# A two-layer decoder trunk whose stages overlap by token pair: the last gate/up pieces run for one pair first, and norms, pool mixer and sums of a pair run in the other pair's products

## The reference

```python
def modulate(x, g, mod):
    shift, scale, gate = jnp.split(mod, 3, axis=-1)
    h = rmsnorm(x, g) * (1.0 + scale[:, None, :]) + shift[:, None, :]
    return h, gate[:, None, :]
...
#   x += 1/2 * gate * SwiGLU_1(h);  x += gate * Mixer_l(h);  x += 1/2 * gate * SwiGLU_2(h)
def swiglu(h, w_in, w_out):            # D_FF = 2816
    g, u = jnp.split(h @ w_in, 2, axis=-1)
    return (jax.nn.silu(g) * u) @ w_out
...
def mixer_pool(h, w_grp, scale):       # layer 1; 4 channel groups, windows 2, 4, 8, 16
    ...
        p = ((cg - prev) / cnt).astype(h.dtype) - h[..., sl]   # trailing mean minus the token itself
        outs.append(p @ w_grp[i])
    return jnp.concatenate(outs, axis=-1) * scale
```

## Time and profile before

| | us |
|---|---|
| three runs | 2209.69, 2346.18, 2266.74 |
| median of the three | 2266.74 |
| the profiled execution | 2222.29 |
| its span on the slowest core (7) | 2220.7 |
| its span on core 3, the shortest | 2178.5 |
| busy on core 7: PE, DVE, ACT, POOL | 2081.5, 1314.5, 749.5, 609.8 |

### The profile page before, as it was taken

One profiled execution on the slowest core, in us unless ns is written; L12 is line 12 of the kernel. 1 busy time (PEld: TensorE's weight loads), 2 busy tenths in 40 slices (PEclk: granted clock), 3 DMA queues, 4 the chain that ended last, 5 costly groups with the idle time before them and its releaser, 6 DMA issues.

```text
span 2220.7 us, 30634 instructions; the slowest of 8 cores (2178.5 to 2220.7 us)
## 1 busy us (share of the span) xinstructions
PE 2081.5 (94%) x9537; PEld 930.7 (42%) x9537; DVE 1314.5 (59%) x2222; ACT 749.5 (34%) x1186; POOL 609.8 (27%) x602
## 2 busy tenths in 40 slices
PE   7999999999999899999998999999976599999996
PEld 1344444445534344444443444444433244444443
DVE  1664665666777675575766765656555554444446
ACT  2630321355225630230347311303234632130333
POOL 0041340501102052250520431423535334052320
PEclk9999999999999999999999999999988799999998
DMA  9443361542342064371450551533400024023123
GB/s 275 116 99 63 95 142 31 130 87 39 75 118 55 13 140 86 76 142 34 119 105 1 115 123 44 123 72 86 76 1 1 10 39 76 1 48 57 29 48 152
DMA packets 65438, 174.60 MB, mean 79 GB/s; under 512 B 6912, under 2 KB 7040, under 8 KB 63872
## 3 DMA queue, kind: packets, MB, share of 16 engines
q0 software_dynamic: 21744, 79.18, 21.1%
q1 hardware_dynamic: 43536, 93.46, 13.9%
HBM read 243.39 MB, written 8.39 MB: 113 GB/s over the span
## 4 chain that ended last, share of the span: by engine, by line
PE 80%; DVE 7%; issue 5%; ACT 5%; DMA 2%; POOL 1%; SPq 1%; DVEq 0%; ACTq 0%; POOLq 0%
PE ps L253 80%; DVE TP L253 4%; ACT TP L253 1%; ACT TSUM L253 1%; DMA ACTB<-wm 1%; ACT H L253 1%; DVE X L253 1%; DVE ACTB L253 1%; DVE TSUM L253 1%; DVE WMOD L253 1%; ACT L253 1%; SPq L253 1%; DMA WMOD<-wmod 1%; DVE ps L253 0%; POOL CB L253 0%
## 5 line engine op out<-in xcount | busy, mean ns | idle before, releaser
L253 PE MATMUL ps<-H,SLIN 128*128 128x512 f16 x2240 | 554.2, 393 | 18.6 <-DVE ps L253 12.8
L253 PE MATMUL ps<-ACTB,SLOUT 128*128 128x512 f16 x2368 | 529.0, 384 | 8.4 <-DVE TP L253 4.6
L253 DVE SCALAR_TENSOR_TENSOR X<-ps,GH,X 128x512 f32<-128x512 f32 x448 | 332.6, 749 | 338.7 <-PE ps L253 337.3
L253 PE MATMUL ps<-TSUM,SLIN 128*128 128x512 f16 x2016 | 509.9, 389 | 20.5 <-ACT ps L253 13.1
L253 ACT ACTIVATE TP<-ps 128x512 f32<-128x512 f32 x568 | 337.5, 598 | 402.4 <-PE ps L253 363.1
L253 POOL TENSOR_TENSOR SLIN<-SLIN 128x512 f16<-128x512 f16 x336 | 442.3, 1337 | 105.7 <-DMA SLIN<-wp 47.9
L253 PEld LDWEIGHTS ps<-ACTB,SLOUT 128*128 128x128 f16 x2368 | 233.2, 99 | 294.0 <-issue 37.2
L253 POOL DMA_DIRECT2D SLIN<-wp x91 | 51.0, 561 | 1108.3 <-PE ps L253 1098.5
L253 PEld LDWEIGHTS ps<-H,SLIN 128*128 128x128 f16 x2240 | 223.1, 100 | 306.4 <-issue 94.9
L253 ACT ACTIVATE ps<-ps 128x512 f32<-128x512 f32 x168 | 97.9, 583 | 735.0 <-PE ps L253 728.9
L253 PEld LDWEIGHTS ps<-TSUM,SLIN 128*128 128x128 f16 x2016 | 199.0, 100 | 278.2 <-issue 88.2
(11 more groups left out here) (82 smaller groups left out, 852.8 us busy)
## 6 DMA issues: line engine op xcount, KB each, us to landing
WMOD<-wmod SPq DMA_DIRECT2D x256, 256.0 KB, 4.1
SLIN<-wp POOLq DMA_DIRECT2D x91, 512.0 KB, 6.8
SLOUT<-wp POOLq DMA_DIRECT2D x60, 512.0 KB, 11.7
X<-xT SPq DMA_DIRECT2D x8, 1024.0 KB, 29.3
outT<-ACTB SPq DMA_DIRECT2D x4, 2048.0 KB, 6.3
H<-wm SPq DMA_DIRECT2D x4, 1024.0 KB, 12.0
ACTB<-wm SPq DMA_DIRECT2D x3, 1024.0 KB, 22.5
ACTB<-wm SPq DMA_DIRECT2D x2, 512.0 KB, 23.7
```

What stands on the lines that cost most here:

```text
L253: return lambda E: getattr(E, name)(*a, **k)
```

## The change

The two pairs of tiles are made to overlap across sub-layers.

- The last pieces of the last group (NLATE: 5, 5, 7 and 3 of the 7 for the four FFNs) run for pair 0 first (part l0); then tiles 0 and 1 get their output projection; then the same pieces run for pair 1 (l1, in reverse order where more than three), then tiles 2 and 3. Likewise the first pieces (NEARLY: 5, 5 and 8) of the FFNs but the first run for pair 0 (e0) and then for pair 1 (e1). In (1,2), e0 is the whole first group, and the outputs of tiles 0 and 1 come ahead of e1.
- A piece that is used in both passes is loaded and summed again if a slot was taken from it in between. Chain plans the loads into the three slots over the whole sequence of items and gives up the piece whose next use is farthest. The four FFNs load and sum 101 pieces where 84 were summed before; the SLIN loads become about 112 (91 before), POOL's sums 404 (336).
- What pair 0 needs next (norm, pool mixer, token sums) goes into a queue BG, whose steps run at six hooks in each item of pair 1, and one to three per chunk of the output projection.
- Norms: squares by 128x1024, rstd kept in TSUM, the product with rstd by 128x1024 into the input's place, then scale and shift in place, half on ACT and half on DVE.
- Pool mixer: X is cast to f16 by eight DMAs on POOL's queue; the norm's scale goes into the weights and rstd into the copy of the grouped product; the statistics come from ACT's squares and matmuls of one column. The shift of (1,1), which the pooling cancels but for rounding, is not computed: 16 of 256 w_mod steps go. POOL's 64 squares go.
- The final norm is written in place and stored by two chunks (512 KB each).
- In the middle group three w_mod steps stand in an item, and none while BG holds work. The four SLOUT loads are issued ahead of l0, not at its end.

The diff, cut to its core:

```diff
+    class Chain:
...
+            fut = self.seq[idx:]
+
+            def use(p):
+                return fut.index(p) if p in fut else 10 ** 6
...
+            for p in fut:
+                if p in seen:
+                    continue
+                seen.append(p)
...
+                        break
+                    self.drop(v)
+                slot = self.free.pop(0)
+                self.res[p] = slot
+                load_piece(p, slot, after)
+                self.pend.append(p)
+                if len(seen) > 4:
+                    break
+            for p in old:
+                self.pend.remove(p)
+                s_sums(p)
+
+        def drop(self, p):
+            self.free.append(self.res.pop(p))
+            piece_slot.pop(p, None)
...
 
     def mod_step():
+        if mod_next[0] == 96:
+            mod_next[0] = 104
...
-    def rstd_from(b, rs=None, tmr=None):
...
+    def rstd_ops(ts, bs):
+        for t, b in zip(ts, bs):
+            rs, k = rs_of(t)
+            add("act", I("activation", out=rs, in_=PS[b][:], func=AF.Ln, scale=1.0 / D, bias=EPSB[:, 0:1]),
+                reads=[("ps", b), "EPSB"], writes=k)
+            BK.give(b)
+        for t in ts:
+            rs, k = rs_of(t)
+            add("act", I("activation", out=rs, in_=rs, func=AF.Exp, scale=-0.5), reads=k, writes=k)
+
+    def stat_units(t):
+        sq_pair(t, 0)
+        yield
+        sq_pair(t, 2)
+        yield
+        sq_pair(t, 4)
...
-    def apply_gen(l, s, t, rs, tmr=None):
+        ones_pair(t, 0, b)
+        sq_pair(t, 6)
+        yield
+        ones_pair(t, 2, b)
+        yield
+        ones_pair(t, 4, b)
+        yield
+        yield
+        ones_pair(t, 6, b)
+        return b
...
+    def apply_units(l, s, t, nact):
...
+        rs, rk = rs_of(t)
+
+        def norm(c):
+            add("dve", I("tensor_tensor", out=role.hbuf[:, c:c + 2, tsl(t)], in0=X[:, c:c + 2, tsl(t)],
+                         in1=rs.unsqueeze(1).broadcast_to([128, 2, TT]), op=ALU.mult),
+                reads=[Xk(c, t), Xk(c + 1, t)] + rk, writes=[(role.hn, c, t), (role.hn, c + 1, t)])
+
+        def aff(x):
+            v = role.hbuf[:, x, tsl(t)]
+            k = (role.hn, x, t)
+            if (x * nact) % 8 < nact:
+                add("act", I("activation", out=v, in_=v, func=AF.Identity, scale=AS[:, o + x:o + x + 1], bias=MODT[:, sh + x:sh + x + 1]),
+                    reads=[k, ("AS", l, s), ("MODF", l, s)], writes=[k])
+            else:
+                add("dve", I("tensor_scalar", out=v, in0=v, scalar1=AS[:, o + x:o + x + 1], scalar2=MODT[:, sh + x:sh + x + 1],
+                             op0=ALU.mult, op1=ALU.add), reads=[k, ("AS", l, s), ("MODF", l, s)], writes=[k])
+        for c in range(0, NC, 2):
+            norm(c)
             yield
+            aff(c)
+            aff(c + 1)
+            yield
+
+    def head_units(l, s, ts, nact=4):
+        bs = []
+        for t in ts:
+            b = yield from stat_units(t)
+            bs.append(b)
+        rstd_ops(ts, bs)
+        yield
+        yield
+        for t in ts:
+            yield from apply_units(l, s, t, nact)
 
     def tv(p, n, c):
...
                 hook()
                 g.p7()
                 if mod:
...
+                if mod and nmod > 2:
+                    mod()
                 hook()
                 self.prev = g
 
...
-    def ffn_prefetch(l, i, n=3):
...
-    NEARLY = 3
...
+    NEARLY = {(0, 2): 5, (1, 0): 5, (1, 2): 8}
+    NLATE = {(0, 0): 5, (0, 2): 5, (1, 0): 7, (1, 2): 3}
...
+            ne = NEARLY[(l, s)]
+            P["e0"] = one(l, s, 0, range(ne), 0)
+            P["e1"] = one(l, s, 0, reversed(range(ne)) if ne > 3 else range(ne), 1)
+            P["g0"] = both(l, s, 0, range(ne, n0))
+        P["g1"] = both(l, s, 1, range(len(GROUPS[1])))
+        P["g2"] = both(l, s, 2, range(n2 - nl))
+        P["l0"] = one(l, s, 2, range(n2 - nl, n2), 0)
+        P["l1"] = one(l, s, 2, reversed(range(n2 - nl, n2)) if nl > 3 else range(n2 - nl, n2), 1)
...
+    def wout_load(l, s, g):
+        for dp in range(4):
+            load_piece(("wout", l, s // 2, g, dp), 3 + dp)
...
+    def out_t(l, s, t, g, nu, split=False):
...
+        for dch in range(d0, NC):
+            b = BK.take()
+            mms(dch, b, order)
+            post(dch, b)
+            PIPE.flush()
+            BG.step(nu)
...
+        def mod():
+            if BG.q:
+                return
+            if mod_next[0] < (72 if (l, s) == (0, 0) else 144):
+                mod_step()
+            elif (l, s) == (1, 0):
+                next(pm_const_ops, None)
...
+        pairs = not P["g0"]
+        if P["e0"]:
+            cut = len(P["e0"]) - (4 if pairs else 0)
+            PIPE.run(P["e0"][:cut], BG.step)
+            if pairs:
+                wout_load(l, s, 0)
+                PIPE.run(P["e0"][cut:], BG.step)
                 mod_finalize_gate(l, s)
-            if g < 2:
-                for t in range(NT):
...
+                for t in (0, 1):
+                    out_t(l, s, t, 0, 3, t == 0)
+            BG.drain()
+        PIPE.run(P["e1"], BG.step, mods)
+        if pairs:
+            for t in (2, 3):
+                out_t(l, s, t, 0, 1, t == 2)
+        else:
+            split = max(0, len(P["g0"]) - 4)
+            PIPE.run(P["g0"][:split], BG.step, mods)
+            wout_load(l, s, 0)
+            PIPE.run(P["g0"][split:], BG.step, mods)
+            mod_finalize_gate(l, s)
+            for t in range(NT):
+                out_t(l, s, t, 0, 1)
+        for g in (1,):
+            PIPE.run(P["g1"][:10], BG.step, mods, 3)
+            wout_load(l, s, 1)
+            PIPE.run(P["g1"][10:], BG.step, mods, 3)
+            for t in range(NT):
+                out_t(l, s, t, 1, 1)
+        PIPE.run(P["g2"], BG.step, mods)
+        wout_load(l, s, 2)
+        PIPE.run(P["l0"][:-2], BG.step, mods)
+        nxt.prep()
+        PIPE.run(P["l0"][-2:], BG.step, mods, quiet=True)
+        nu = 3 if (l, s) == (1, 0) else 2
+        for t in (0, 1):
+            out_t(l, s, t, 2, nu, t == 0)
+            nxt.ready(t)
+        PIPE.run(P["l1"], BG.step, quiet=True)
+        for t in (2, 3):
+            out_t(l, s, t, 2, nu, t == 2)
+            nxt.ready(t)
...
-    def pm_core_gen(l, s, t):
...
+    def pool_units(p):
+        ts = (2 * p, 2 * p + 1)
+        for t in ts:
+            for h in range(2):
+                cs = slice(4 * h, 4 * h + 4)
+                add("pool", I("dma_start", out=H[:, cs, tsl(t)], in_=X[:, cs, tsl(t)]),
+                    reads=[Xk(c, t) for c in range(4 * h, 4 * h + 4)], writes=[Hk(c, t) for c in range(4 * h, 4 * h + 4)], dma=("PX", t, h))
...
+            ss(i)
+            if i + 2 < 8:
+                sq(i + 2)
+            yield
...
-    def pm_stage2(tail_fn, ln, sn):
...
-    def final_apply_gen(t, rs):
...
+    def final_units(t):
+        b = yield from stat_units(t)
+        rstd_ops([t], [b])
+        rs, rk = rs_of(t)
         for c in range(NC):
-            add("dve", I("scalar_tensor_tensor", out=Ov[ob][:, c, :], in0=X[:, c, tsl(t)], scalar=SM[:, SM_FG + c:SM_FG + c + 1],
-                         in1=TP[:, rs, 0:TT], op0=ALU.mult, op1=ALU.mult),
-                reads=[Xk(c, t), "SM", ("TP", rs)], writes=[("O", ob, c)] + O_KEYS[ob])
-            yield
-        add("sp", I("dma_start", out=outT_v[t], in_=Ov[ob][:]), reads=[("O", ob, c) for c in range(NC)] + O_KEYS[ob], dma=("OUT", ob))
+            add("dve", I("scalar_tensor_tensor", out=X[:, c, tsl(t)], in0=X[:, c, tsl(t)], scalar=SM[:, SM_FG + c:SM_FG + c + 1],
+                         in1=rs, op0=ALU.mult, op1=ALU.mult),
+                reads=[Xk(c, t), "SM"] + rk, writes=[Xk(c, t)])
+            if c % 2:
+                add("sp", I("dma_start", out=outT_v[t][:, c - 1:c + 1, :], in_=X[:, c - 1:c + 1, tsl(t)]),
+                    reads=[Xk(c - 1, t), Xk(c, t)], dma=("OUT", t, c))
+                yield
...
+    class ToFfn:
...
+            l, s = self.l, self.s
+            ro = role_of(l, s)
+            if t == 1:
+                BG.add(("h", 1), head_units(l, s, (0, 1)))
+                BG.add("T0", t_sums_gen(ro.hbuf, ro.hn, 0))
+            elif t >= 2:
+                BG.add(("h", t), head_units(l, s, (t,)))
+                if t == 3:
+                    BG.add("T1", t_sums_gen(ro.hbuf, ro.hn, 1))
+                    BG.need("T0")
...
+    class ToPool:
...
+        def ready(self, t):
+            if t % 2:
+                p = t // 2
+                ro = role_of(1, 2)
+                BG.add(("p", p), pool_units(p))
+                if n_sub_run > 5:
+                    BG.add(("h", t), head_units(1, 2, (t - 1, t)))
+                    BG.add("T%d" % p, t_sums_gen(ro.hbuf, ro.hn, p))
+            if t == 3:
+                BG.need("T0")
+
```

More of the change, by code:

```diff
@@ L757, in __init__, with run @@
             self.prev = None
-        def run(self, items, hook, after, mod=None):
+        def run(self, items, hk, mods=None, nmod=2, quiet=False):
```

(17 more changed lines are left out.)

640 lines of the change are left out of this document (303 added, 337 removed).

## The result

The changed kernel is slower: 2278.3 us (median of four runs, 2270.3 lowest) against 2238.3 for the kernel before in the same comparison (2209.7 lowest); the ratio is 1.031, with a 95% interval of 1.024 to 1.038. The ratio leaves out executions in which a die took clearly longer at a lower clock, and so differs from that of the medians. The forecast was 2200, with a range of 2130 to 2275.

A forecast was written before the change was run, and what follows sets the result against it. The prediction took PE's work plus its waits and slower running as the bound, with 151 us lost in four stretches. New costs of 133 less 4 of PE work gave 129, a gain of 22 from 2222.3: 2200 us, range 2130 to 2275.

The forecast's parts named there:

- (ii): Norms inside items: seven rstd with table switches on ACT, 4.1 us of PE wait each, 29 us (0 to 38).
- (v): Middle group, three w_mod steps per item: the few steps that meet output weights cost 8 us (0 to 10).
- (i): Output weights loaded ahead of late pieces: PE waits for those pieces, 46 us in all (0 to 56).
- (iii): First pair's norms and token sums beside (1,0)'s last output tile: DVE's work shows as 8 us (0 to 15).
- (vi): Pool mixer spread over 15 items: 1 us lost per item, 15 us (0 to 62).
- (iv): Pair 1 of the early pieces: reloads and their sums on POOL cost 9 us (3 to 10).
- (vii): The end: smaller last store and final products stored as they come take 3.5 off 17.6 us, leaving 14.
- (viii): Clock: after a long wait of (i) the granted clock may drop for a while, 4 us.
- R2: Rival, chance .13: background work queued in order on ACT and DVE is the bound, 3 us per unit, 2259 us.
- R3: Rival, chance .07: fuller PE brings granted clock .93 throughout instead of .952, 49 us, so 2250 us.
- R4: Rival, chance .04: pool units come too late, the mixer's chain keeps 75 of its 97 us, 2260 us.
- R1: Rival, chance .34: loads and norms hide, (i) is 10 us and (ii) half, 2140 us.

The follow-up runs named there:

- nohead: Changed kernel without the last tile's norm ahead of (0,2) and (1,0), its token sums reading an older input: 2212.0 us on undisturbed cores, against 2247.8 for the changed kernel.
- nosum2: Changed kernel with POOL making a piece's four sums only at its first load, not at reloads: 2225.7 us on undisturbed cores, ratio 1.026.
- best: Changed kernel with later output-weight loads, two w_mod steps per middle-group item and the missing steps in output projections: 2156.8 us on undisturbed cores, ratio 0.979.

## Why the prediction was wrong

The forecast was a gain of 22 us, and 64 were lost on like cores. The step that failed is the price of background work laid into items: norms (ii and the struck-out seams) and w_mod steps (v). I priced each by the one gap that a row showed, where the runs show whole stretches losing 10 to 15 us. The step on late loads was right.

- **(i) right.** Waits of 16.6, 16.3 and 8.4 us in the three passes and 4.9 in (1,2)'s first group, 46.2 against 46. The reading that carried it was from POOL's order: what stands ahead of the load, and when PE first asks for it.
- **The pool mixer, (iii), (vi): right in sum.** -59 against -60; that it is this close is in part luck, since the 4 us of PE work that I booked apart fall there too, and no run separates (vi) from the norms of (ii). DVE's burst before (1,2) is there: waits of 7.9 and 2.0 us for token sums against 8. The granted clock of the stretch rose from .91 to .96, as the signs asked. The 256-column matmuls came down from a mean of 347 ns to 279 only, where the sign was 110 to 200, though they hardly wait any more (0.9 us against 29.2):

```profile
L253 PE MATMUL ps<-CB,H 128*128 128x256 f16 x128 | 19.5, 279 | 0.9 <-DVE TP L253 0.5 <-ACT TP L253 0.4
```

- **The first groups: wrong, 25 us.** Here the reasoning failed, and not the size alone. The forecast struck out the whole 15.5 and 20.6 us of the two seams and put one rstd each back, 4.1. But the last tile's norm stayed where it had been, in the first items of the next product, and nohead shows that this norm is two thirds of what the groups lose now, 12 of 18 and of 20 us. The 4.10 us of the earlier trace rows was one gap among those that made up the 15.5; I priced a norm by one visible gap instead of by the stretch that holds one.
- **(ii): right mechanism, mis-sized.** For the same reason: a pair-1 pass loses 10.0 us in (0,0), 44.0 - 158 x .2143 = 10.1 in (0,2) and 26.4 - 94 x .2143 = 6.3 in (1,2), instead of 4.1. In the first two half is DVE slowed by POOL's sums, which the change itself brings there by reloading pieces (nosum2). I had counted the 68 added sums on POOL alone, as cost of a queue (iv), and not as a load on DVE.
- **(v): right mechanism, mis-sized, 31 us.** 39 instead of 8. I took the few steps that meet the output weights. Before the change DVE was busy for 61.6 of the 85.6 us of a middle group (core 3); with three steps an item it has 71 us of work in 84, each late transfer delays all DVE work behind it, and I didn't add up what the items now hold. In (1,0) half of the loss is another thing that I had not in the sum, the mixer's constants behind a late piece.
- **(vii): no gain.** The end loses 44.7 - 129 x .2143 = 17.1 us on core 7, where 14 was forecast and before has 17.6. The stores land in 3.1 us instead of 6.4, half and not a quarter, and PE now waits 2.7 and 2.1 us for ACT's squares of the last tile.
- **(viii) too small.** Matmuls at half rate behind long waits, and at the starts, cost some 42 us on core 7 where core 3 of before has 26 (512-column matmuls that begin 400 to 440 ns after the one before, less .2143 us each): 16 more, and I had 4.
- **The range of my own case** was added up wrong: the bounds that it names give 2171 to 2219, not 2178 to 2232. Neither holds the result.
- **The rivals.** R2 ended on the right side, slower, and named the right queues, DVE's and ACT's. At 3.5 us per unit its sum would even give the measured time, but by luck: the cost sits in fewer places and is larger in each, and the middle groups, the largest miss, were no part of its 37 units. R3 did not happen: an undisturbed core has .967 against .971, and the stretches at .81 came in both kernels. Its ground was one of them: in the window of the earlier trace rows that has .93 on core 7, core 3 has 1.00 with the same work. R4 did not happen either: ACT's 22.6 us are gone and the stretch is 59 us shorter. R1 had put .34 on loads and norms that hide; they don't.

## What to carry to other kernels

Before work moves into a dense stretch, price it by a whole stretch that already holds such work, loss per unit, and not by one gap of its timeline; and count every engine's load per item, since what is moved off one engine's gap meets in-order queues on the others. A step that prefetches at a faster rate is safest where its engine idles: here the third w_mod step costs 12 to 14 us in the middle groups of (0,0) and of (0,2), and in best the same steps lengthen no output projection of these groups by as much as 0.1 us. A load's order within its queue is worth tens of microseconds: loads that are needed later go behind those that are needed first. And a late load reaches further than the engine that uses it: in (1,0)'s middle group it held PE for 7 us by way of POOL's and DVE's queues.
